# Expert weights in rows of 7 KB through a ring of twelve places, with the feed-forward columns dealt to the array by remainder

## The reference, cut to what matters

```python
def swiglu(x, w_gate, w_up, w_down):          # 1024x3584, 1024x3584, 3584x1024
    return (jax.nn.silu(x @ w_gate) * (x @ w_up)) @ w_down

def moe_swiglu(x, router, w_gate, w_up, w_down):
    logits = (x @ router).astype(jnp.float32)
    top_val, top_idx = lax.top_k(logits, TOP_K)               # TOP_K = 2
    top_w = jax.nn.softmax(top_val, axis=-1)
    combine = jnp.sum(jax.nn.one_hot(top_idx, N_EXPERTS) * top_w[..., None], axis=-2)
    out = jnp.zeros_like(x)
    for e in range(N_EXPERTS):                                # N_EXPERTS = 8
        out = out + combine[..., e:e + 1] * swiglu(x, w_gate[e], w_up[e], w_down[e])
    return out
```

## Time and profile before

| | us |
|---|---|
| median of 3 runs | 3071.53 (3070.17 to 3072.4) |
| the profiled execution, its time | 3074.8 |
| the profiled execution, its span | 3073.1 |
| TensorE busy in the span | 2680.9 |
| experts (first gate product to last down product) | 1998.1 to 3009.5 |

### The profile page before, as it was taken

The page is one execution under the profiler, slowest core; times in us unless marked ns, Lnnn a source line. Parts: engine busy times, 40 slices in busy tenths (PEclk is TensorE's granted clock), DMA queues, the critical chain, the costliest instruction groups (busy, mean ns, idle before and its releaser), DMA issues.

```text
span 3073.1 us, 44267 instructions
## 1 busy us (share of the span) xinstructions
PE 2680.9 (87%) x19827; PEld 1478.5 (48%) x19827; DVE 709.8 (23%) x1246; ACT 472.6 (15%) x757; POOL 126.2 (4%) x320
## 2 busy tenths in 40 slices
PE   8798789899688876799998886699999999999997
PEld 7555346656343465444444475434434344343443
DVE  3423422323521256100001355300000000000002
ACT  2411221411220322100001312100000000000001
POOL 3011000011000020000000020000000000000000
PEclk9899899899899955899999955799999999999998
DMA  7212223222223410244434500199999999999992
GB/s 222 81 63 97 82 82 124 96 73 83 96 82 116 131 43 1 69 150 150 147 117 139 151 1 0 60 334 339 360 343 350 349 336 353 350 345 360 339 354 90
DMA packets 293374, 542.33 MB, mean 176 GB/s; under 512 B 28432, under 2 KB 179120, under 8 KB 293168
## 3 DMA queue, kind: packets, MB, share of 16 engines
q1 hardware_dynamic: 279872, 536.95, 50.6%
q10 hardware_dynamic: 12992, 1.22, 0.3%
q0 software_dynamic: 304, 1.05, 0.1%
HBM read 538.12 MB, written 1.05 MB: 175 GB/s over the span
## 4 chain that ended last, share of the span: by engine, by line
PE 52%; DVE 3%; ACT 2%; issue 2%; DVEq 0%; ACTq 0%; PEldq 0%
PE psum L1997 19%; PE psum L335 12%; PE psum L2013 10%; PE psum L1774 3%; PE psum L1617 1%; PE psum L1986 1%; PE psum L1978 1%; PE psum L383 1%; PE psum L2008 1%; PE psum L954 0%; ACT area L963 0%; DVE area L1722 0%; PE psum L945 0%; PE psum L938 0%; DVE area L1720 0%
## 5 line engine op out<-in xcount | busy, mean ns | idle before, releaser
L335 PE MATMUL psum<-ring,hT 128*128 128x512 f32 (+3 forms) x2176 | 921.4, 578 | 70.9 <-ACT xn L538 34.0
L335 PEld LDWEIGHTS psum<-ring,hT 128*128 128x128 f32 x2176 | 399.6, 194 | 519.8 <-issue 432.6
L1997 PE MATMUL psum<-ring,area 128*32 128x448 f32 x6144 | 598.1, 550 | 31.2 <-issue 28.8
L1997 PEld LDWEIGHTS psum<-ring,area 128*32 128x32 f32 x6144 | 198.7, 112 | 422.1 <-issue 422.1
L2013 PE MATMUL psum<-ring,area 128*32 128x256 f32 x5376 | 296.5, 379 | 0.0
L2013 PEld LDWEIGHTS psum<-ring,area 128*32 128x32 f32 x5376 | 172.0, 110 | 117.5 <-issue 6.6
L460 PE MATMUL psum<-hT,ring 128*128 128x256 f32 x768 | 167.4, 380 | 0.0
L460 PEld LDWEIGHTS psum<-hT,ring 128*128 128x128 f32 x768 | 146.4, 191 | 21.0 <-issue 1.0
L2135 DVE TENSOR_TENSOR area<-area,psum 128x1344 f32<-128x1344 f32 x16 | 24.9, 1555 | 436.5 <-PE psum L1997 436.5
L1617 PE MATMUL psum<-area 32*128 32x128 f32 (+1 forms) x448 | 98.0, 400 | 12.9 <-DVE area L1566 10.4
L1617 PEld LDWEIGHTS psum<-area 32*128 32x128 f32 (+1 forms) x448 | 89.3, 300 | 20.7 <-DVE area L1566 10.6
(11 more groups left out here) (443 smaller groups left out, 2075.2 us busy)
## 6 DMA issues: line engine op xcount, KB each, us to landing
ring<-in_moe_w_gate_dram SPq DMA_DIRECT2D x128, 896.0 KB, 7.5
ring<-in_moe_w_up_dram SPq DMA_DIRECT2D x128, 896.0 KB, 7.3
ring<-in_w_in_dram SPq DMA_DIRECT2D x96, 1024.0 KB, 5.0
ring<-in_moe_w_down_dram SPq DMA_DIRECT2D x128, 512.0 KB, 4.9
ring<-in_moe_w_down_dram SPq DMA_DIRECT2D x64, 384.0 KB, 5.5
ring<-in_w_out_dram SPq DMA_DIRECT2D x16, 1024.0 KB, 5.0
ring<-in_moe_w_down_dram SPq DMA_DIRECT2D x64, 256.0 KB, 5.0
ring<-in_ffn_w_gate_dram SPq DMA_DIRECT2D x14, 1024.0 KB, 5.0
```

The costliest lines, as they stand in the source:

```text
L335: last = nc.tensor.matmul(acc(g)[:, t, 0:d["n"]], lhs(kk, t), w[:, k, :], start=kk == 0, stop=kk == d["nk"] - 1)
L1997: last = nc.tensor.matmul(PS[32 * j:32 * j + 32, 3 * (q % 2) + b, 0:PIECE], XG[:, k, 32 * b:32 * b + 32], expert_slot(8 * q + k, PIECE * j ...
```

## The change

- The ring has twelve places. The four new ones lie at the end of `area`, the buffer for intermediate results (columns 15552 to 22719); to make room `SGE` goes, and silu's result is written straight into `HE` and multiplied there. The loads of the four new places wait for the end of the mixer's use of `area` (`mix_ready`).
- `freed_before` searches back for the last load whose place overlaps, instead of working it out by cases.
- Each expert load is one row of 1792 contiguous values (7 KB) for each partition: half a row of gate or up, and for down a sixteenth of the 28 contiguous rows that a partition now has. There are 48 loads for each expert.
- Instead of four passes there are two, `wide(e, 0, ...)` for gate and `wide(e, 1, ...)` for up, over sixteen tiles each. Product `j` of the four reads columns `j`, `j+4`, `j+8`, ... of the tile. Gate's results stand in banks 0 to 5 and up's follow in the same banks, after silu has read them. In the first pair of tiles the second half goes first.
- `turn` takes every seventh column of `HE` (`c::7`), so that a chunk belongs to the down rows that the partitions now hold.
- `gather(e + 1)` comes straight after the up products instead of after the third down part; it signals after each half, and `evacuate` takes one half at a time. All transposes come after it: two, then down part 0, two, part 1, two, part 2, one, parts 3 to 6.
- The scatters come after 6 and 12 of the 16 gate tiles. ScalarE does both silus first and then copies `PWE`.
- TensorE counts a down tile as used with its last product rather than at the end of a chunk.

```diff
-MOE_RING = 8
+MOE_RING = 12
...
+        def expert_part(e, j):
+            if j < 32:
+                q, k, half = j // 16, j % 16 // 2, j % 2 if j > 1 else 1 - j
+                v = A[("moe_w_gate_2", "moe_w_up_2")[q]].rearrange("x e (k p) n -> p (x e k) n", p=P)
+                return (expert_slot(j, 0, MOE_SLOT).rearrange("p (a n) -> p a n", a=1),
+                        v[:, bass.ds(e * KD + k, 1), MOE_SLOT * half:MOE_SLOT * half + MOE_SLOT])
+            v = A["moe_w_down_2"].rearrange("x e (p i) n -> p (x e) (i n)", p=P)
+            c = MOE_SLOT * (j - 32)
+            return expert_slot(j, 0, MOE_SLOT).rearrange("p (a n) -> p a n", a=1), v[:, bass.ds(e, 1), c:c + MOE_SLOT]
...
+            def wide(e, q, k0, k1):
+                for k in range(k0, k1):
+                    for i, p in enumerate((1, 0) if (q, k) == (0, 0) else (0, 1)):
+                        slot = 16 * q + 2 * k + i
+                        expert_landed(pe, r, e, slot)
+                        if (q, k) == (1, 0):
+                            pe.wait_ge(ms("sg"), 2 * e + (p + 1) + r * PASS["sg"])
+                        for b in range(BLOCKS):
+                            if (q, k, p) == (0, 0, 0):
+                                pe.wait_ge(ms("YE"), 3 * e + (b + 1 + r * PASS["YE"]))
+                            for j in range(4):
+                                last = nc.tensor.matmul(PS[32 * j:32 * j + 32, 3 * p + b, 0:PIECE],
+                                                        XG[:, k, 32 * b:32 * b + 32],
+                                                        expert_slot(slot, j, MOE_SLOT - j, 4),
+                                                        start=k == 0, stop=k == KD - 1)
+                        last.then_inc(sem(("weights_used", "o_used", "o_used")[r]), 1)
...
             def turn(e, c):
-                pe.wait_ge(ms("h"), 2 * e + (1 if c < 3 else 2) + r * PASS["h"])
-                if c >= 2:
+                if c == 0:
+                    pe.wait_ge(ms("h"), 2 * e + 2 + r * PASS["h"])
+                if c < 2:
+                    pe.wait_ge(ms("XG"), 2 * e + (c + 3 + r * PASS["XG"]))
+                else:
                     pe.wait_ge(ms("HT"), 7 * e + (c - 1) + r * PASS["HT"])
                 for b in range(BLOCKS):
-                    last = nc.tensor.transpose(PS[:, 6 + c % 2, b * P:(b + 1) * P], HE[:, b, c * P:(c + 1) * P], IDENT)
+                    last = nc.tensor.transpose(PS[:, 6 + c % 2, b * P:(b + 1) * P], HE[:, b, c::7], IDENT)
...
             with pe.Fori(0, NE) as e:
-                pe.wait_ge(ms("XG"), e + 1 + r * PASS["XG"])
-                piece(e, 0)
+                pe.wait_ge(ms("XG"), 2 * e + (2 + r * PASS["XG"]))
+                wide(e, 0, 0, 3)
                 pe.wait_ge(ms("PWE"), e + 1 + r * PASS["PWE"])
                 pe.wait_ge(ms("YT"), e + 1 + r * PASS["YT"])
                 scatter(0)
-                piece(e, 1)
+                wide(e, 0, 3, 6)
                 pe.wait_ge(ms("added"), 2 * e + 1 + r * PASS["added"])
                 scatter(1)
-                pe.wait_ge(ms("sg"), 2 * e + 1 + r * PASS["sg"])
-                piece(e, 2)
+                wide(e, 0, 6, 8)
+                wide(e, 1, 0, 8)
                 pe.wait_ge(ms("added"), 2 * e + 2 + r * PASS["added"])
-                for c in range(3):
-                    turn(e, c)
-                piece(e, 3)
-                pe.wait_ge(ms("sg"), 2 * e + 2 + r * PASS["sg"])
+                gather(e + 1)
+                turn(e, 0)
+                turn(e, 1)
                 down(e, 0)
+                turn(e, 2)
                 turn(e, 3)
+                down(e, 1)
                 turn(e, 4)
-                down(e, 1)
                 turn(e, 5)
+                down(e, 2)
                 turn(e, 6)
-                down(e, 2)
-                pe.wait_ge(ms("HT"), 7 * e + 7 + r * PASS["HT"])
-                gather(e + 1)
                 down(e, 3)
                 down(e, 4)
                 down(e, 5)
                 down_last(e)
```

More of the change, by code:

```diff
@@ L281, in blocks_kernel, with place @@
             LANDED.append(counts[slot_of(n)])
-        assert PER_EXPERT % MOE_RING == 0 and RING * HALF == MOE_RING * MOE_SLOT
-        def freed_before(n):
[L286 to L292, removed]
+        assert PER_EXPERT % MOE_RING == 0
+        def place(n):
+            if not MOE0 <= n < MOE1:
+                return slot_of(n) * HALF, HALF
+            return (n - MOE0) % MOE_RING * MOE_SLOT, MOE_SLOT
+        def freed_before(n):
+            a, w = place(n)
+            m = n - 1
+            while m >= 0 and not (place(m)[0] < a + w and a < sum(place(m))):
+                m -= 1
+            return m + 1
         def group(name, L):
@@ L1887, in down_chunk @@
-        def down_chunk(i):
-            return 7 * (i % 4) + i // 4
-        PER_SLOT = [sum(16 * len(expert_parts(0, j)) for j in range(i, PER_EXPERT, MOE_RING)) for i in range(MOE_RING)]
-        def expert_landed(eng, r, e, j):
[L1894 to L1899, removed]
+        MORE = AREA - (MOE_RING - RING * HALF // MOE_SLOT) * MOE_SLOT
@@ L1981, in gather @@
                                                 start=t == 0, stop=t == 1)
-                last.then_inc(ms("gather"), 1)
+                    if k % 4 == 3:
+                        last.then_inc(ms("gather"), 1)
             def scatter(t):
@@ L1988, in scatter @@
                 last.then_inc(ms("scatter"), 1)
-            def piece(e, q):
-                for k in range(KD):
-                    expert_landed(pe, r, e, 8 * q + k)
-                    for b in range(BLOCKS):
-                        if q == 0 and k == 0:
-                            pe.wait_ge(ms("YE"), 3 * e + (b + 1 + r * PASS["YE"]))
-                        for j in range(4):
-                            last = nc.tensor.matmul(PS[32 * j:32 * j + 32, 3 * (q % 2) + b, 0:PIECE],
-                                                    XG[:, k, 32 * b:32 * b + 32],
-                                                    expert_slot(8 * q + k, PIECE * j, PIECE),
-                                                    start=k == 0, stop=k == KD - 1)
-                    last.then_inc(sem(("weights_used", "o_used", "o_used")[r]), 1)
@@ L2016, in down_matmul, with down_landed @@
                                         start=i == 0, stop=i == 27)
+                if b == 2 and flat % 7 == 6:
+                    last.then_inc(sem(("weights_used", "o_used", "o_used")[r]), 1)
+                return last
+            def down_landed(e, i):
+                for flat in range(4 * i, 4 * i + 4):
+                    if flat % 7 == 0:
+                        expert_landed(pe, r, e, 32 + flat // 7)
             def down(e, c):
@@ L2093, in pass_act @@
             with act.Fori(0, NE) as e:
-                def gate(p):
-                    expert_used(act, r, e, 16 * p + 8)
-                    if p:
-                        act.wait_ge(ms("h"), 2 * e + 1 + r * PASS["h"])
-                    nc.scalar.activation(SGE, PS[:, 0:3, 0:PIECE], ACT.Silu).then_inc(ms("sg"), 1)
-                gate(0)
+                for p in range(2):
+                    expert_used(act, r, e, 15 + p)
+                    nc.scalar.activation(HE[:, :, PIECE * p:PIECE * p + PIECE], PS[:, 3 * p:3 * p + 3, 0:PIECE], ACT.Silu)\
+                        .then_inc(ms("sg"), 1)
                 act.wait_ge(ms("scatter"), 2 * e + 2 + r * PASS["scatter"])
```

102 lines of the change are left out of this document (44 added, 58 removed).

## The result

The changed kernel takes 3697.44 us (median of 4 executions, 3694.71 to 3702.7) where the kernel before, run beside it, takes 3071.97 (4 executions, 3070.17 to 3074.92). The ratio is 1.2037, its 95% interval 1.2016 to 1.2058. The forecast was 3065 in a range up to 3680: wrong in sign and in size, and outside its own range by 17 us. What came is the mechanism of rival B.

A forecast was written before the change was run, and what follows sets the result against it. TensorE was taken to bound the kernel, with loads hidden; 8 x (-0.14 - 0.75) = -7.1, +1 for the refill, gave -6 us, 3065 against the median 3071.53, range 3056 to 3680.

The forecast's parts named there:

- rival B: Gate and up products: the strided read sets TensorE's pace; 3400 to 3790 us, middle 3540; chance 0.30.
- What bounds the kernel: Expert stage: TensorE's own pace, 376 ns a step of 448 columns; loads hidden, no weight arrives late; 127.19 us an expert.
- Rows of 7 KB, ring of twelve: Expert loads: longer rows and four more places are worth 0, as no product waits for a landing.
- the refill: Turn of the expert loop: code packets fetched again stand between 7 KB rows; at most +3 us, taken as +1.
- Order of the passes: Gate and up products: two passes joined, one boundary less, -0.14 us an expert; activations and scatters hidden.
- gather ahead: Gather before the transposes covers their 1.07 us stall; both together 7.02 instead of 7.77 us, -0.75 an expert.
- The stall: Second group of transposes waits for the evacuation of gather's second half: 0.3 us, 0.75 with the ceiling.
- Columns by remainder: Products reading every fourth column and transposes every seventh cost 0, by the block inversion's row.
- Its middle price: Strided gate and up products with VectorE's added time, 0.69 ns a column over 1536 steps: +473 us.
- Its top price: Strided gate and up products with VectorE's whole time, 1.88 ns a column instead of 0.83: +720 us.
- C: Small prices: transposes +15 us with free products, 3080; with gather's stall and the refill up to 3086; chance 0.08.
- D: Down loads lose rate from contiguous pieces 112 KB apart: 3260 us; decides below 260 GB/s in the down part; chance 0.05.

The follow-up runs named there:

- x_blocks: The changed kernel, but gate and up products read blocks of 448 contiguous columns; transposes stay at every seventh column: 3060.21 us, ratio 0.9962.
- x_mended_ring8: x_mended with a ring of eight places instead of twelve: 3057.4 us, ratio 0.9951.
- x_blocks_both: x_blocks with the transposes also reading 128 contiguous columns: 3057.62 us, ratio 0.9958.
- x_mended: The changed kernel computing the reference with products and transposes reading in a row, down tiles loaded as rows of up to 4 KB: 3054.35 us, ratio 0.9947.
- x_step2: The changed kernel with all four products reading every second column instead of every fourth: 3095.54 us.
- x_old_turn7: The kernel before with only the transposes taking every seventh column: 3076.18 us, ratio 1.0013.
- x_old_stride4: The kernel before with only its gate and up products reading every fourth column: 3700.64 us.

## Why the prediction was wrong, step by step

**What bounds the kernel:** right. TensorE's own pace, with loads hidden behind it: in x_blocks with its rows of 7 KB, and in x_mended_ring8 with its shallower ring, no product waits for a landing.

**Rows of 7 KB, ring of twelve, 0 (+1 for the refill):** right as to 0 for the ring (x_mended_ring8); for the rows no run stands by itself, but x_blocks_both adds up without a term for them. The refill didn't get longer; the idle turn became shorter, 3.37 to 3.5 us on average instead of 4.12 in the changed kernel, x_blocks and x_blocks_both (3.89 in x_mended). Why is open; no run separates it.

**Order of the passes, gather ahead:** right in the gather, not in the boundary. The -0.14 an expert for one boundary less didn't come: in x_blocks_both the products of gate and up take 72.58 us an expert outside the slow clock, before 72.60. The stall was put at 0.3 us and is 0.28 in the timeline above; VectorE's evacuation of half the gather at 0.55 and is 0.56, as its timeline shows:

```profile
2365.93 0.56 DVE L2121 TENSOR_TENSOR area<-psum,param_cols 128x384 f32<-128x384 f32 x1 [0.38 <-PE psum L1969]
...
2367.72 0.56 DVE L2121 TENSOR_TENSOR area<-psum,param_cols 128x384 f32<-128x384 f32 x1 [1.23 <-PE psum L1969]
```

Gather and transposes take 7.47 us an expert. The forecast said 7.02, and x_blocks_both takes 7.02; the 0.45 between them is the spaced weight load, which lengthens a group of six transposes from 0.81 to 0.94 and which I had put at 0.

**Columns by remainder, "I take 0, by the row that is nearest":** this is the step that failed. The strided read of the products was put at no price, from the earlier trace rows, and it costs 415 ns in each of 1536 steps, 637 us. The recorded reading of that row is that a fresh 16 bytes every 1.83 ns costs nothing; the change needs one every 0.83 ns. A row that shows no price at 1.83 ns bounds the price from above and says nothing of any value under it, and the price turned out to be 1.78. The bound itself was also read too tightly. Other products of the same block inversion, all of 64 columns in a row, show it in TensorE's timeline of the kernel before:

```profile
162.95 1.15 PE L680 MATMUL psum<-area 64*64 64x64 f32 x32
164.03 1.98 PE L335 MATMUL psum<-ring,hT 128*128 128x512 f32 x4
...
197.41 1.14 PE L702 MATMUL psum<-area 64*64 64x64 f32 x16
198.48 1.98 PE L335 MATMUL psum<-ring,hT 128*128 128x512 f32 x4
```

L680 alternates between two tiles on the array's diagonal, L702 stays in one. The records come every 34 ns in the first (1.08 us for 32) and every 67 ns in the second (1.07 for 16), and 64 columns at two clocks are 53 ns: so the two tiles run side by side. The products of the earlier trace rows alternate in the same way. Each of their two streams then had 2 x 29.3 = 58.6 ns for its 16 pieces, one every 3.7 ns and not every 1.83, and the row bounds the price at 3.7 ns only. What sets the 29.3 ns isn't known; it isn't the read, since 32 columns in a row take the same. To be nearest in engine and type was no argument. The other row, on another engine, did show a price for reads far apart, and I gave it a chance of 0.30. "TensorE takes half of what the array could take" was an argument from the array, not from the memory's read.

**Rival B:** right in mechanism, mis-sized. Measured over whole experts are 795 - 378 = 417 ns a step, times 1536 = +640, less the 1.69 us of slow clock that eight first passes no longer lose: +626. Its middle price (+473) added VectorE's 0.69 ns to the array's 0.83, as if the two times followed each other; they lie side by side, and the longer decides. Its top price put VectorE's whole mean, 1.88 ns a column, in the place of the array's, and that was the right form, but the mean includes what an instruction costs however long it is. Two sizes of the same instruction in the kernel before, groups of VectorE's instructions, take that out:

```profile
L986 DVE TENSOR_REDUCE small<-area 128x8 f32<-128x2048 f32 x6 | 13.7, 2286 | 0.2
...
L1155 DVE TENSOR_REDUCE area<-area 128x256 f32<-128x2048 f32 x2 | 7.4, 3686 | 0.1
L1155 DVE TENSOR_REDUCE area<-area 128x128 f32<-128x1024 f32 x2 | 3.8, 1913 | 0.1
```

L1155 sums values far apart: (3686 - 1913)/1024 = 1.73 ns for each value. In a row (L986 here and in the earlier trace rows, a maximum) it is (2286 - 1220)/1024 = 1.04. The two also differ in what they give out, one value for every eight and one for every 128 or more, and no row sums eight in a row, so that part of the difference may belong to that. With 1.73 in place of the array's 0.83, rival B's sum is 1536 x (448 x 1.73 - 376) = +613, which on the forecast's 3065 gives 3678, 19 us under what came. These figures stood in the trace of before; that TensorE would pay nearly the same for a value as VectorE stood in none, and the closeness is in part luck.

**The range.** Its upper end of 3680 takes in "a doubling of the strided products", +573, but not rival B's top price of +720, although B's whole span of 3400 to 3790 had the chance of 0.30. The truth lay in the part left out.

**The Trainium skill.** "SBUF — State Buffer", section "Door 1: The DMA port swizzle", says in one note that a line is 16 bytes and wants two hits, and in its next sentence that four float32 is as far as one strides for free. The runs agree with the first: with two columns in each 16 bytes (x_step2) a step takes 400 ns against 376, almost free, with one (the changed kernel) 797. They contradict the second: a stride of three already takes 604 ns, and four is the full price.

**C and D.** C's small price exists (x_old_turn7, about +4 us of at most 15). D is refuted: down products take 380 ns, no landing ends a wait. (Its bound of 260 GB/s for the down part doesn't follow from its own numbers, 14.7 MB in 127.19 - 29.4/0.388 = 51.4 us, which is 286.)

## What to carry to other kernels

Before an operand's columns are spaced out, count how many of them fall into each 16 bytes and multiply the pieces by what one costs. On this engine that was 1.78 ns for the moving operand; where only another engine has such a row, its slope from two sizes of one instruction is a better guess than a mean (here 1.73). Then take the larger of that and the array's time. A row that is itself limited by something else only bounds a price and never shows that it is zero, and before its pace is read, count how many streams share it. And where a loop with a long body shows idle "issue" time at each turn with a slow clock behind it, write it out: here that was worth 40 us, more than twice what the whole rest of the change could give.

## What was not expected of the hardware

The price for each fresh 16 bytes is even: 1.78 ns, taken from spacing 4, predicts spacings 2 and 3 within 1%. Four streams that run side by side don't divide it among them, so that one spaced stream of four costs as much as four.

While the read sets the pace, the slow clock costs almost nothing. In the window 2208 to 2212 the granted clock is 0.57, that is for the most part its lower level of 1.2 GHz, and yet the first section of 36 steps takes 2236.20 - 2207.47 = 28.73 us. The one that starts at 2411.13 has a granted clock of 1.00 and takes 28.55: the slow clock costs 0.2 us here, where it costs 1.69 when columns are read in a row. (In x_old_stride4 a first pass takes 38.44 us, the others 37.8 to 38.3.) At 1.2 GHz the array would need 448 x 2 clocks = 747 ns, still less than the read.

An idle turn of nearly the same length is sometimes followed by the slow clock and sometimes not: in x_blocks_both after 3.30 us it was, after 3.15 us not, and after 3.68 us (at 2869.96, 13.74 us) not either. What decides between them is open.
